# Memory attention: values of two query blocks multiplied together, from high and low halves, in place of fp32 products per block

## What is computed

```python
def _memory_cross_attention(h, m, w_q, w_kv, w_o):
    q = _heads(jnp.einsum('bsd,dc->bsc', h, w_q), N_MEM_HEADS)
    kv = jnp.einsum('bmd,dc->bmc', m, w_kv)
    k, v = jnp.split(kv, 2, axis=-1)
    k, v = _heads(k, N_MEM_HEADS), _heads(v, N_MEM_HEADS)
    logits = jnp.einsum('bhqd,bhkd->bhqk', q, k) * (MEM_HEAD_DIM ** -0.5)
    p = jax.nn.softmax(logits, axis=-1)
    o = jnp.einsum('bhqk,bhkd->bhqd', p.astype(v.dtype), v)
    return jnp.einsum('bsc,cd->bsd', _merge(o), w_o)
```

## Time and profile before

| | |
|---|---|
| median of 3 runs | 1944.24 us (1943.66 to 1944.81) |
| the profiled execution | 1944.89 us |
| its span | 1942.7 us |
| TensorE products, busy | 1921.1 us |
| VectorE, busy | 1464.8 us |
| ScalarE, busy | 893.6 us |
| memory attention | 370 to about 433 us |

### The profile page before, as it was taken

The page is one execution under the profiler, slowest core; times in us unless marked ns, Lnnn a source line. Parts: engine busy times, 40 slices in busy tenths (PEclk is TensorE's granted clock), DMA queues, the critical chain, the costliest instruction groups (busy, mean ns, idle before and its releaser), DMA issues.

```text
span 1942.7 us, 26034 instructions
## 1 busy us (share of the span) xinstructions
PE 1921.1 (99%) x10345; PEld 1637.4 (84%) x10345; DVE 1464.8 (75%) x2031; ACT 893.6 (46%) x1395; POOL 161.0 (8%) x184
## 2 busy tenths in 40 slices
PE   9999999999999999999999999999999999999998
PEld 7887777888899999888888899988878888888886
DVE  6665687569867788736477888887898788887787
ACT  5454464326454455523323444434467654434443
POOL 1001350000011110000000010000024300000000
PEclk9999999999999999999999999999999999999999
DMA  5322212215498884333223323332223132332321
GB/s 178 109 87 66 91 62 87 87 39 157 130 239 221 214 216 130 106 102 96 87 87 103 120 88 106 112 109 66 77 69 100 44 120 82 116 107 88 107 66 65
DMA packets 163511, 210.58 MB, mean 108 GB/s; under 512 B 10944, under 2 KB 120128, under 8 KB 163392
## 3 DMA queue, kind: packets, MB, share of 16 engines
q1 hardware_dynamic: 150752, 190.63, 30.5%
q0 software_dynamic: 11008, 16.80, 5.1%
q10 hardware_dynamic: 1632, 1.51, 0.2%
HBM read 198.41 MB, written 2.10 MB: 103 GB/s over the span
## 4 chain that ended last, share of the span: by engine, by line
PE 87%; DVE 7%; ACT 2%; DMA 2%; issue 1%; POOL 0%; SPq 0%; ACTq 0%; DVEq 0%; POOLq 0%
PE bank L898 17%; PE bank L900 16%; PE bank L899 16%; PE bank L1508 5%; PE bank L1509 5%; PE bank L1507 5%; PE bank L1071 4%; PE bank L950 2%; PE bank L952 2%; PE bank L951 2%; PE bank L1356 2%; PE bank L1358 2%; PE bank L1360 2%; DMA arena<-w_up 2%; PE bank L1063 2%
## 5 line engine op out<-in xcount | busy, mean ns | idle before, releaser
L898 PE MATMUL bank<-h_hi,w_hi 128*128 128x512 f32 x1128 | 446.4, 396 | 2.0 <-DVE w_lo L1657 1.2
L900 PE MATMUL bank<-h_hi,w_lo 128*128 128x512 f32 x1128 | 439.6, 390 | 0.0
L899 PE MATMUL bank<-h_lo,w_hi 128*128 128x512 f32 x1128 | 439.2, 389 | 0.0
L898 PEld LDWEIGHTS bank<-h_hi,w_hi 128*128 128x128 f32 x1128 | 211.9, 188 | 48.8 <-issue 3.1
L899 PEld LDWEIGHTS bank<-h_lo,w_hi 128*128 128x128 f32 x1128 | 211.9, 188 | 44.5 <-issue 2.1
L900 PEld LDWEIGHTS bank<-h_hi,w_lo 128*128 128x128 f32 x1128 | 211.7, 188 | 44.6
L2718 ACT ACTIVATE w_hi<-raw 128x1024 fp32r<-128x1024 f32 (+3 forms) x159 | 155.1, 1011 | 197.6 <-PE bank L900 139.9
L1657 DVE TENSOR_TENSOR w_lo<-raw,w_hi 128x1024 fp32r<-128x1024 f32 (+2 forms) x147 | 179.3, 1248 | 19.6 <-ACT w_hi L2718 19.4
L898 PE MATMUL bank<-g_hi,w_hi 128*128 128x512 f32 (+1 forms) x460 | 177.9, 387 | 3.9 <-DVE resid L1719 1.0
L900 PE MATMUL bank<-g_hi,w_lo 128*128 128x512 f32 (+1 forms) x460 | 172.6, 375 | 0.0
L899 PE MATMUL bank<-g_lo,w_hi 128*128 128x512 f32 (+1 forms) x460 | 172.3, 375 | 0.0
(11 more groups left out here) (346 smaller groups left out, 4083.1 us busy)
## 6 DMA issues: line engine op xcount, KB each, us to landing
raw<-w SPq DMA_DIRECT2D x32, 1024.0 KB, 5.4
arena<-w SPq DMA_DIRECT2D x32, 1024.0 KB, 5.1
arena<-w_up SPq DMA_DIRECT2D x56, 512.0 KB, 5.9
raw<-a_w_in SPq DMA_DIRECT2D x16, 1024.0 KB, 5.3
raw<-w_in SPq DMA_DIRECT2D x11, 1024.0 KB, 5.2
raw<-w_down SPq DMA_DIRECT2D x11, 1024.0 KB, 7.5
raw<-w_mkv SPq DMA_DIRECT2D x8, 1024.0 KB, 5.3
arena<-w_up POOLq DMA_DIRECT2D x16, 512.0 KB, 8.8
```

The costliest lines, as they stand in the source:

```text
L898: nc.tensor.matmul(dst, a_hi, b_hi, start=(k == 0), stop=False)
L899: nc.tensor.matmul(dst, a_hi, b_lo, start=False, stop=False)
L900: last = nc.tensor.matmul(dst, a_lo, b_hi, start=False, stop=(k == n - 1))
```

## The change

Values are multiplied for two units together, from halves. `mem_v` is split once into `mem_value_hi` and `mem_value_lo` (two copies on ScalarE and two subtractions on VectorE, beside the query projection). Each unit's turned probabilities are split as they leave `pt_bank`: ScalarE's copy writes `mem_prob_hi` and counts `mem_prob_high`; VectorE then subtracts it from the bank into `mem_prob_lo`, and it is this subtraction that counts `pt_taken`. TensorE skips the values at even units and does both units of a pair at the odd one, with 256 moving columns.

```diff
+        mem_value_hi, mem_value_lo, mem_prob_hi, mem_prob_lo = [in_arena(*which) for which in (
+            ("mem_value_hi", 8192, 2048), ("mem_value_lo", 10240, 2048), ("mem_prob_hi", 17408, 1024), ("mem_prob_lo", 20480, 1024))]
...
+        mem_value_halves = [t.rearrange("p (k n) -> p k n", n=D) for t in (mem_value_hi, mem_value_lo)]
+        mem_prob_halves = [t.rearrange("p (b k n) -> p b k n", b=2, n=256) for t in (mem_prob_hi, mem_prob_lo)]
+        def mem_prob_of(t, u):
+            return t[:, u // 2 % 2, :, P * (u % 2):P * (u % 2) + P]
...
@@ TensorE, attention
-                    if 0 <= v < n and (v % 4 == 3 or not in_fours):
+                    if 0 <= v < n and (v % 4 == 3 or not in_fours) and (kind != "mem" or v % 2):
...
-                        if v % per == 3 * in_fours:
+                        if v % per == 3 * in_fours or kind == "mem":
                             pe.wait_ge(o_taken, first_group + v // per)
...
+                        elif kind == "mem":
+                            if v == 1:
+                                pe.wait_ge(mem_value_ready, MT)
+                            values(h, i, [t[:, u // 2 % 2, :, :] for t in mem_prob_halves]).then_inc(pv_done, 2)
...
-            def mem_values(h, i, pt):
-                return several([(o_bank[:, 256 * j + P * (i % 2):256 * j + P * (i % 2) + P],
-                                 mem_v[:, k, 256 * h + P * j:256 * h + P * j + P], pt[:, P * k:P * k + P],
-                                 k == 0, k == 1) for j in range(2) for k in range(2)])
+            def mem_values(h, i, prob_halves):
+                (v_hi, v_lo), (p_hi, p_lo) = mem_value_halves, prob_halves
+                ops = []
+                for j in range(2):
+                    dst, cut = o_bank[:, 256 * j:256 * j + 256], slice(256 * h + P * j, 256 * h + P * j + P)
+                    for k in range(MT):
+                        ops += [(dst, v_hi[:, k, cut], p_hi[:, k, :], k == 0, False),
+                                (dst, v_hi[:, k, cut], p_lo[:, k, :], False, False),
+                                (dst, v_lo[:, k, cut], p_hi[:, k, :], False, k == MT - 1)]
+                return several(ops)
...
@@ VectorE, attention, behind the reduction
+                    if kind == "mem" and 0 <= s - lag < n:
+                        u = first + s - lag
+                        dve.wait_ge(mem_prob_high, s - lag + 1)
+                        p_hi, p_lo = [mem_prob_of(t, u) for t in mem_prob_halves]
+                        V.tensor_tensor(p_lo, pt_bank[:, 0:NMEM].rearrange("p (k n) -> p k n", n=P), p_hi.bitcast(F32),
+                                        ALU.subtract).then_inc(pt_taken, 1)
...
@@ VectorE, query projection, after tile n was taken
+                if n in (2, 4):
+                    k = n // 2 - 1
+                    dve.wait_ge(mem_value_high, k + 1)
+                    V.tensor_tensor(mem_value_halves[1][:, k, :], mem_v[:, k, :], mem_value_halves[0][:, k, :].bitcast(F32),
+                                    ALU.subtract).then_inc(mem_value_ready, 1)
...
@@ ScalarE, attention
+                        if kind == "mem":
+                            act.wait_ge(pv_done, max(first, u - u % 2 - 2))
+                            A(mem_prob_of(mem_prob_halves[0], u), pt_bank[:, 0:nk].rearrange("p (k n) -> p k n", n=P),
+                              ACT.Copy).then_inc(mem_prob_high, 1)
...
@@ ScalarE, ahead of the query projection's pieces
-            for _ in range(3):
+            split_high()
+            for k in range(MT):
+                A(mem_value_halves[0][:, k, :], mem_v[:, k, :], ACT.Copy).then_inc(mem_value_high, 1)
+            for _ in range(2):
                 split_high()
```

More of the change, by code:

```diff
@@ L303, in build @@
         pt_taken = sem("pt_taken")
+        mem_prob_high = sem("mem_prob_high")
+        mem_value_high = sem("mem_value_high")
+        mem_value_ready = sem("mem_value_ready")
         pv_done = sem("pv_done")
@@ L2795, in attention @@
                         back_by = 4 if kind in four_prob_t else 2
-                        if u >= back_by:
-                            act.wait_ge(pv_done, u - back_by + 1)
-                        A(prob_t_of(kind, u)[:, 0:nk], pt_bank[:, 0:nk], ACT.Copy).then_inc(pt_taken, 1)
+                        if kind == "mem":
+                            act.wait_ge(pv_done, max(first, u - u % 2 - 2))
+                            A(mem_prob_of(mem_prob_halves[0], u), pt_bank[:, 0:nk].rearrange("p (k n) -> p k n", n=P),
+                              ACT.Copy).then_inc(mem_prob_high, 1)
+                        else:
+                            if u >= back_by:
+                                act.wait_ge(pv_done, u - back_by + 1)
+                            A(prob_t_of(kind, u)[:, 0:nk], pt_bank[:, 0:nk], ACT.Copy).then_inc(pt_taken, 1)
                     if s < n:
```

## The result

The changed kernel takes 1947.01 us (median of 20 runs, 1945.6 to 1950.94), the kernel before 1944.37 us (20 runs). The ratio is 1.0014 with a 95% interval of 1.0008 to 1.0021: slower by 2.6 us, inside what I had called no change, and clear of noise over this many runs. The forecast was +1.7 us.

A forecast was written before the change was run, and what follows sets the result against it. TensorE, nearly always busy, was taken to bound the kernel. Short steps +3.4 us and later pairs -1.7 sum to +1.7, giving a 1945.9 us median; forecast's own range 1944.9 to 1947.6, overall range 1942.9 to 1948.6.

The forecast's parts named there:

- the sixth turn: Last of six probability transposes in memory attention's short steps, at 386.51 us before; forecast 3.4 us late.
- The product's price: Value products on halves: 0.120 us each, 12 per pair, 1.44 us against 1.78, saving 0.34 per pair.
- that rival: Weight loads of the value products show: 0.188 us per product, 6.5 us more, 1952.4 us; chance 0.12.
- The subtraction's price: VectorE's new 128x256 subtraction out of the bank, 16 times: 0.42 us each, bounds 0.35 and 0.48.
- From turn to the next dependent instruction: TensorE's turn through copy and subtraction: 1.41 us after, 0.95 before; against 1.11 of work, 0.30 short per short step.
- Steps 4 to 9: Memory attention's short steps, walked over three queues: first to sixth turn 13.7 us against 9.94, so 3.4 us late.
- The three places where a queue stands ahead: Work queued ahead of the subtraction or its copy at pairs 1, 2 and 3: 0.87, 0.34 and 1.12 us.
- After step 9: Projection steps: 3.87 us of work hides the 1.41 us wait; five remaining pairs give back 1.7 us.
- The value halves: One-time split of mem_v beside the query projection: costed at nothing, up to 2.4 us if its cover were gone.
- The rival in which the subtraction is hidden: Subtraction hidden as the copy was, only 8 x 0.34 us saved: -2.7, 1941.5 us; chance 0.15.

The follow-up runs named there:

- late pieces sooner: Changed kernel with low halves of the third projection chunk's weight pieces made in VectorE steps 14 and 15 instead of 15 and 16; 1945.97 us.
- early pieces later: Changed kernel with low halves of the second chunk's weight pieces made in VectorE steps 9 and 10 instead of 3 and 4; 1946.75 us.
- no subtraction: Changed kernel without the probability-halves subtraction: ScalarE's copy releases TensorE, and low-half products take the high half instead; 1942.00 us.
- subtraction only: Kernel before, plus VectorE's subtraction into an unread scratch tile, counting the semaphore TensorE waits on; values stay fp32, unit by unit; 1949.02 us.
- both moves: Changed kernel with low halves of weight pieces in VectorE steps 9, 10, 14 and 15 instead of 3, 4, 15 and 16; 1944.95 us.
- turn first: Changed kernel with TensorE's turn (two transposes of a unit's probabilities) ahead of the pair's values in each memory attention step; 1944.87 us.
- turn first, both moves: Changed kernel with TensorE's turn ahead of the values, and weight-piece low halves in VectorE steps 9, 10, 14 and 15; 1943.17 us.
- and late tile halves: As "turn first, both moves", with ScalarE making the first two projection tiles' high halves behind unit 5's copy instead of ahead; 1942.63 us.
- value halves only: Kernel before, plus only the unread copies and subtractions of mem_v; 1944.54 us against 1944.41.
- fastest: As "and late tile halves", with second chunk's weight pieces later: high halves in ScalarE steps 9 and 10, low in VectorE steps 10 and 11; 1942.14 us.
- moves only: Kernel before with only the weight pieces placed as in "fastest" (ScalarE 9, 10; VectorE 10, 11, 14, 15); 1944.36 us against 1944.41.

## Why the prediction was right, and where it was not

| kernel | stretch, walked | stretch, measured | median over before |
|---|---|---|---|
| changed | 88.3 (forecast), 89.3 (with the wait for the piece) | 89.32 | +2.6 |
| late pieces sooner | 88.2 | 88.23 | +1.6 |
| early pieces later | 88.4 | 88.46 | +2.4 |
| no subtraction | 84.7 | 84.78 | -2.4 |
| subtraction only | 90.7 | 91.01 | +4.7 |
| both moves | 87.3 | 87.38 | +0.5 |
| turn first | 87.2 | 87.14 | +0.5 |
| turn first, both moves | 85.9 | 85.94 | -1.2 |
| and late tile halves | 85.5 | 85.27 | -1.8 |
| value halves only | 86.6 | 86.61 | +0.1 |
| fastest | 84.7 | 84.50 | -2.3 |
| moves only | 86.3 | 86.32 | -0.1 |

The medians follow the stretches within 0.6 us. That is far inside their intervals, about 1.7 us either way, so the finer steps of this table rest on the stretches alone.

*The total.* The measured +2.6 lies in the stated range. But that range was drawn for the prices of the subtraction and of a product, and both came out as taken; what it covered was a term that I had not thought of. In this the forecast was lucky. By parts the stretch has +3.25 up to the sixth turn (forecast 3.4), -1.64 after it (forecast -1.7; from the run with the late pieces sooner) and +1.09 for the weight piece (forecast nothing).

*The product's price.* 0.120 us was taken from the MLP, 0.118 to 0.120 is what stands here. The estimate of 109 ns that the prediction works out from the Trainium skill (TensorE: Matmul & The Clock Gate, section "Wait — 56ns, not 53.3ns?") is not what this kernel shows. The load records are 0.19 us long here as well and are hidden; that rival had its chance and is out.

*The subtraction's price.* 0.42 us was taken from a group with other operands (a multiplication, though the prediction calls it subtract-like); the new group of the changed kernel, next to the copy that now writes the high half, reads:

```profile
L1814 DVE TENSOR_TENSOR mem_prob_lo<-bank,mem_prob_hi 128x256 fp32r<-128x256 f32 x16 | 6.8, 423 | 11.0 <-ACT mem_prob_hi L2831 11.0
...
L2831 ACT ACTIVATE mem_prob_hi<-bank 128x256 fp32r<-128x256 f32 x16 | 6.1, 382 | 32.5 <-PE bank L1079 32.5
```

*From turn to the next dependent instruction.* 1.41 us walked, 1.40 measured.

*Steps 4 to 9.* The walk had the sixth turn 19.9 us after the first score product, it came at 19.80. The three places where a queue stands ahead are those seen. Counted from start to start, the first product of a pair comes 2.17, 1.63 and 2.42 us after the turn, where 1.40 is the plain distance: 0.77, 0.23 and 1.02 us for what stands ahead, where the prediction had 0.87, 0.34 and 1.12. From that product to the next turn it is 1.53 to 1.54 us, where it had 1.44, since a first product that had to wait stands 0.22 us and not 0.12 ahead of the second. So three terms were 0.1 too large and three 0.1 too small, and they cancel in the sum. The brackets in the lists are shorter than the waits from start to start, which explains the 3.3 us listed where the prediction had about 4. Moving the weight pieces took 0.82 us off the sixth turn (0.87 in the prediction), moving the tile halves 0.67 off the stretch (0.4 by the walk, with the turn first). The Trainium skill (TensorE: Matmul & The Clock Gate, section "Architectural detail: the array is 16× 32×32, not 1× 128×128") calls ScalarE and VectorE strict first-in-first-out; these moves show what that means here, in microseconds.

*After step 9.* This step failed. The prediction says that between a turn and the next values 3.87 us stand against 1.41 and that VectorE's 0.33 us per step fall "in a stretch where it is half idle". Both are so, and the five pairs do give 0.33 us each (1.64 in all). But I asked only whether TensorE waits for the *subtraction*, and left out of the walk what else stands in VectorE's queue behind it and has a due time: the weight piece of step 16, ready 0.66 us early before, 1.0 us late after. It was the term left out of the sum: 1.09 of the 2.70 us, by the run with the late pieces sooner. Half idle on the average (54% busy in the earlier trace rows) is no margin for the one instruction that is due, and the new instruction's own wait, 1.64 us in step 15, counts as idle too while it holds up all that stands behind it.

*The value halves.* Costed at nothing; measured at nothing.

*The attribution.* The subtraction alone costs 4.4 us in the stretch. The products alone, released by the copy, save 1.84 us in the stretch. That they do not save 2.7 is read from its turns: where 2.55 us of work stand between two turns (0.22 + 0.89 + 1.44), they are 3.07 us apart over the third pair (383.00 to 386.07; the copy of unit 5 stands behind the tile halves), 2.76 over the first and 2.63 over the second, 0.8 us in all. The rival in which the subtraction is hidden had -2.7 us; even with no subtraction at all the kernel gained 2.4 us by the medians and 1.8 by the stretch.

## What to carry to other kernels

When an instruction is put between a producer and the engine that sets the end, walk all queues step by step with prices from the rows, and give the walk every wait of the engine that sets the end, those for weights included; a queue that is half idle can still be late for one due instruction, and the inserted instruction brings its own wait into that queue. Work that another engine must do before a hand-over goes behind independent work in the order: swapping two blocks of TensorE's program took 2.2 us off the stretch here, four fifths of what the change had cost, and 1.4 where the weight pieces had been moved already. And where the effect is near the spread of the medians, measure it as the distance between two fixed instructions of the trace.

## What I had not expected

The place of the memory attention in the span moves by 4 us between executions of programs that are the same up to there. In the execution of the kernel with the early pieces later, the first input arrived late; from its timeline, and from that of the changed kernel:

```profile
8.96 0.66 PE L1120 MATMUL bank<-ident,arena 128*128 128x128 f32 x4 [2.36 <-DMA arena<-x]
```

```profile
6.51 0.66 PE L1120 MATMUL bank<-ident,arena 128*128 128x128 f32 x4 [0.52 <-DMA arena<-x]
```

That is 2.5 of the 4.1 us between their first score products (373.28 and 369.17). In the same execution the granted clock of the first 60 us was 0.97 instead of 1.00, so for a part of them it was at 1.2 GHz and not at 2.4: products with 512 columns stand 0.43 us apart there (11.44 to 11.87), 0.23 in the changed kernel (8.13 to 8.36). The rest of the 4.1 us fits that, but was not tried apart. A single span of this kernel can therefore not show a change of 2 us, while a distance inside the trace repeats within a few hundredths in the two cases that can be compared: the stretch is 86.62 us before and 86.61 with the value halves only, and the sixth turn came 19.80 us after the first score product both in the changed kernel and in the one with the late pieces sooner (370.00 to 389.80).
